# One hybrid decoder layer on one core: expert weights as 384 units in one ring of twenty buffers, experts written out

## The chip, the cores and the metric

The kernel runs on one core of a Trainium2 chip. The metric is the device time of one execution in microseconds, smaller being better. A profiled execution gives the trace from which the rows below are copied.

## The reference, cut to what matters

320 tokens (256 of a prompt, 64 new ones) of width 1024 go through one layer. A projection to seven parts of 1024 columns feeds two recurrent branches, whose merged result goes through `w_out` and a layer norm. Then a router picks 4 of 32 experts for each token, and a second layer norm closes the layer. Everything is float32. Each expert has a gate-and-up matrix of 1024 x 2048 (8 MB) and a down matrix of 1024 x 1024 (4 MB), so the 32 experts bring 384 MB from memory.

```python
proj = x @ w_in + b_in                       # 7 parts
... # two convolutions, a gated linear recurrence, gates
x = layernorm(ALPHA * x + mixed @ w_out, ln1_g, ln1_b)
top_vals, top_idx = lax.top_k(x @ router_w + router_b, 4)
gates = softmax(top_vals)
# for each expert e and each token row that chose it
gu   = xb @ w_gu[e] + b_gu[e]
gate = minimum(gu[:, :1024], 7.0)
up   = clip(gu[:, 1024:], -7.0, 7.0)
h    = (up + 1.0) * (gate * sigmoid(1.702 * gate))
y    = h @ w_down[e] + b_down[e]             # added to the token with its gate
x = layernorm(ALPHA * x + y_sum, ln2_g, ln2_b)
```

## The kernel before, in words

**Projection.** The first stage (0 to 230 us) makes 56 pieces of 128 output columns. A piece `q` is loaded (`raw`), rounded by ScalarE (`split_high`, L439), its remainder is taken by VectorE (`split_low`, L795), and TensorE multiplies it in three passes (L604). Seven pieces make a block `c` of 128 channels, and VectorE does the convolutions and the recurrence of the block in the same program order. There are four buffers of a piece. The product with `w_out` (L622) and the first norm follow, then the router.

**Experts.** Work comes in items: one expert with at most 64 rows. An expert with more rows gives more items; with these inputs there are just 32. A loop `one_pair(p)` runs over pairs of items on TensorE, VectorE and ScalarE, with the expert read from a list `items` by VectorE. For each item TensorE does, in this order:

- 64 matmuls of `w_gu` (L742; eight loads of 1 MB, called k, each used by eight matmuls of 128x512),
- one that spreads the row positions (L747),
- `gather` (L689): the rows of the *next* item, by a one-hot matrix that VectorE made in `pick` (L1016, L1017), after `low_part` (L1071) has taken the last result out of the same bank,
- `turn` (L695): four 128x128 transposes of the gathered rows, between two ScalarE copies (L529, L533),
- `turn_h` (L702): four transposes of the activated rows, reading every second column, then a ScalarE copy (L548),
- between these, `combine` (L710): the previous item's result back to token order, for VectorE to add (L833 with out `x_tok`),
- the bias (L762) and 32 matmuls of `w_down` (L769; four loads of 1 MB), then the next item's bias (L736).

VectorE clamps gate and up out of PSUM into the SBUF tile `mid` (L1088, L1089), ScalarE takes the tanh (L544), VectorE makes the product (L833 on `mid`).

**Weight buffers.** SyncE issues all loads from one queue in program order. There are 19 buffers of 1 MB: ten in `ring_gu`, `ring_last`, and eight in `ring_dn`. Even and odd items share the `ring_gu` buffers of k = 3 to 7 and own those of k = 0 to 2; each parity has four `ring_dn` buffers. `load_pair` issues in a fixed order, and a load whose buffer is not free holds back all behind it:

```python
for s in range(2):
    for k in range(KC) if early and s == 0 else (0, *gu_order[:-OWN], *range(1, OWN)):
        load_gu(experts[s], s, k, before * 16 + (16 + gu_count(0, k) if s == 1 and k >= OWN else
                                                 gu_count(1 if k >= OWN else s, k)))
    for u in range(4):
        sp.wait_ge(dn_used, before * 8 + (4 * s + u + 1))
        load_dn(experts[s], s, u)
```

The biases of all experts are loaded after `w_out` into `mid`, rounded by ScalarE (L502), and their remainder is taken by VectorE (L917) after the last block.

Of the kernel before, what the change touches and what calls it, by code (L numbers as in the profile page):

```python
# [24 lines left out]
OWN = 3  # L25
# [32 lines left out]
K_PAIR = 4  # L58
# [14 lines left out]
def hybrid_layer(nc, x_prompt, x_sample, state_h, state_conv, state_sc, w_in, b_in, conv_a_w,  # L73
# [5 lines left out]
    with ctx:  # L79
# [10 lines left out]
        slot = 8 * D  # L90
        GU, DN = 0, 10 * slot
        XT, X1 = DN + 8 * slot, DN + 8 * slot + 12 * D
        MID = X1 + 12 * D
        MID_SIZE = 4 * 3776
        at = [MID + MID_SIZE + 2 * slot]
# [14 lines left out]
        ring_gu = place("ring_gu", [P, 10, 2 * FF], GU)  # L110
        ring_dn = place("ring_dn", [P, 8, 2 * D], DN)

        def gu_slot(s, k):
            return KC + k if s == 1 and k < OWN else k

        ring_last = place("ring_last", [P, 2 * FF], MID + MID_SIZE + slot)

        def gu_tile(s, k):
            return ring_last[:, :] if gu_slot(s, k) == 10 else ring_gu[:, gu_slot(s, k)]

        gu_order = tuple(range(OWN, KC)) + tuple(range(OWN))

        def gu_count(s, k):

            return 8 * s + gu_order.index(k) + 1

        raw = place("raw", [P, RING, KC, P], DN)  # L130
        w_hi = place("w_hi", [P, RING, KC, P], DN + 2 * slot, F32R)
        w_lo = place("w_lo", [P, RING, KC, P], DN + 4 * slot, F32R)
        dsm = place("dsm", [P, 2 * D], DN + 7 * slot)
# [24 lines left out]
        x_hi = place("x_hi", [P, KC, T], MID, F32R)  # L158
        x_lo = place("x_lo", [P, KC, T], MID + 10 * D, F32R)
        mixT = place("mixT", [P, KC, T], MID + 20 * D)  # L160
# [3 lines left out]
        bias4 = place("bias4", [P, 3, HALF], MID + 28 * HALF, F32R)  # L164
        onehot = place("onehot", [P, 3, ROWS], MID + 20 * D)
        posT4 = place("posT4", [P, T], MID + 20 * D + 12 * ROWS, F32R)

        ident = small_tile("ident", [P, P])
        upper = small_tile("upper", [P, P])
        ones = small_tile("ones", [P, P])  # L170
        iota = small_tile("iota", [P, (NB + 1) * ROWS])
        rw = small_tile("rw", [P, KC, NE])
        esel4 = place("esel4", [P, 2, 2, ROWS], at[0] - 4 * KC * NE, F32R)
        rb = small_tile("rb", [P, NE])
        posm = small_tile("posm", [P, 3, NE])
        gate = small_tile("gate", [P, 3, NE])
        onehotT = small_tile("onehotT", [P, 2, T], F32R)
        where4 = small_tile("where4", [P, 2, NE])
        row_at = small_tile("row_at", [P, NB + 1])
        items = small_tile("items", [1, 2, 64], I32)  # L180
# [9 lines left out]
        tiles = place("tiles", [P, 12 * T + 2 * P], GU + 8 * slot)  # L190
# [18 lines left out]
        xg_sb, xgT_f = (mid[:, i * HALF:(i + 1) * HALF] for i in range(2))  # L209
        ys = place("ys", [P, 2, HALF], MID + 8 * HALF, F32R)  # L210
# [8 lines left out]
        gm, th, up = (mid[:, i * HALF:(i + 1) * HALF] for i in range(4, 7))  # L219
        bias_raw = mid[:, 4 * HALF:7 * HALF]  # L220
        pos4 = mid[:, 2240:2240 + 3 * P].rearrange("p (t a h e) -> p t a h e", t=3, a=2, h=2)
# [18 lines left out]
        oh4 = mid[:, 2240:2624].rearrange("p (t k e) -> p t k e", t=3, k=TOPK)  # L240
        og4 = mid[:, 2624:3008].rearrange("p (t k e) -> p t k e", t=3, k=TOPK)
# [10 lines left out]
        gu_in = [sem(f"gu_in{k}") for k in range(KC + OWN)]  # L252
        dn_in = [sem(f"dn_in{k}") for k in range(8)]
# [20 lines left out]
        gu_used, dn_used = sem("gu_used"), sem("dn_used")  # L274
# [11 lines left out]
        slot_out = ring_dn[:, 0:4, :].rearrange("p j (k n) -> p j k n", k=2)  # L286
        ln_g, ln_b = ring_dn[:, 6, 0:D], ring_dn[:, 6, D:2 * D]
        ln2g, ln2b = ring_gu[:, OWN, 0:D], ring_gu[:, OWN, D:2 * D]
# [3 lines left out]
        def _(sp):  # L292
            def load_piece(q):
                if q >= RING:
                    sp.wait_ge(lo_ok, q - RING + 1)
                col = ORDER[q % 7] * D + (q // 7) * P
                sp.dma_start(raw[:, q % RING], win_v[:, :, col:col + P]).then_inc(raw_in[q % RING], 16)

# [21 lines left out]
            for q in range(4, NP):  # L320
                load_piece(q)
                if q % 4 == 3 and q < 7 + 4 * KC:
                    k = (q - 7) // 4
                    sp.dma_start(ring_gu[:, k], w_gu[0, 0, k * P:(k + 1) * P, :]).then_inc(gu_in[k], 16)
            sp.dma_start(rw[:, :, :], router_w[0].rearrange("(k p) e -> p k e", p=P)).then_inc(misc_in, 16)
            sp.dma_start(rb[:, :], router_b[0:1, :].to_broadcast([P, NE])).then_inc(misc_in, 16)
            sp.dma_start(ln_g, ln1_g[0:1, :].to_broadcast([P, D])).then_inc(ln_in, 16)
            sp.dma_start(ln_b, ln1_b[0:1, :].to_broadcast([P, D])).then_inc(ln_in, 16)
            for j in range(4):
                if j < 2:  # L330
                    sp.wait_ge(lo_ok, NP - 2 + 2 * j)
                else:
                    sp.wait_ge(proj_done, NP - 6 + 2 * j)
                sp.dma_start(slot_out[:, j], wout_v[:, 2 * j:2 * j + 2, :]).then_inc(wout_in[j], 16)
# [9 lines left out]
            def load_gu(e, s, k, used=None):  # L344

                src = w_gu[0, ds(e, 1), k * P:(k + 1) * P, :].rearrange("a p n -> p (a n)")
                if used is not None:
                    sp.wait_ge(gu_used, used)
# [797 lines left out]
```

## Time and profile before

| what | us |
|---|---|
| median of three runs (1245.11 to 1254.6) | 1250.66 |
| the profiled execution's own time | 1256.6 |
| its span, first to last instruction | 1254.8 |
| TensorE busy | 1194.4 |
| VectorE busy | 526.6 |
| ScalarE busy | 254.3 |
| experts' first and last weight matmul | 295.9 to 1228.6 |
| bytes moved | 443.16 MB |

The own time lies 1.8 us above the span. The span has three parts: up to 295.9 us everything ahead of the experts, then the experts, and after 1228.6 us the last sums, the second norm and the stores (26.2 us). TensorE is busy nearly everywhere, but a busy TensorE can be one whose weights arrive just in time, so the stages have to be read one by one.

### The profile page before, as it was taken

To read this page: it belongs to the slowest core of one execution; us is meant where nothing else is said; L and a number is where in the kernel's file an instruction comes from. 1 tells how busy PE (TensorE), PEld (TensorE's weight loads), DVE (VectorE), ACT (ScalarE), POOL (GpSimd) and SP (SyncE) were. 2 spreads that over 40 slices of the span, in tenths; PEclk is the share of its full clock that TensorE was granted. 3 is DMA by queue.
4 is the path that set the end of the run, shared out by engine and by line. 5 is a ranking of instruction groups with operands and counts; after the bars stand their busy time and mean duration, and the time that the engine had idled before them with its cause. 6 is when DMAs were issued, how large, how long until landed. Compare 5 with 4: busy or idle time off the path is not lost.

```text
span 1254.8 us, 16159 instructions
## 1 busy us (share of the span) xinstructions
PE 1194.4 (95%) x5767; PEld 561.0 (45%) x5767; DVE 526.6 (42%) x991; ACT 254.3 (20%) x392; POOL 13.7 (1%) x16
## 2 busy tenths in 40 slices
PE   8999999899999999999999999999999999999992
PEld 7999999455333333333333333333333333333330
DVE  4788788565332233222333322332222233333326
ACT  3555655211111111111111111111111111111111
POOL 1000000000000000000000000000000000000003
PEclk8999999899999999999999999999999999999996
DMA  7666745837799999999999999999999999999991
GB/s 195 200 214 217 214 135 143 286 119 310 310 369 422 421 422 422 422 422 422 422 422 422 422 421 422 422 422 422 421 422 422 422 422 422 422 422 422 422 402 43
DMA packets 120147, 443.16 MB, mean 353 GB/s; under 512 B 10824, under 2 KB 68312, under 8 KB 70974
## 3 DMA queue, kind: packets, MB, share of 16 engines
q1 hardware_dynamic: 120030, 442.69, 88.5%
q8 instruction: 10, 0.16, 0.1%
q10 hardware_dynamic: 96, 0.22, 0.0%
q14 instruction: 11, 0.09, 0.0%
HBM read 441.34 MB, written 1.53 MB: 353 GB/s over the span
## 4 chain that ended last, share of the span: by engine, by line
PE 62%; DMA 14%; DVE 11%; ACT 6%; SPq 3%; issue 3%; DVEq 0%; ACTq 0%
PE PS L742 27%; PE PS L769 15%; DMA ring_gu<-in_w_gu 13%; PE PS L689 6%; PE PS L604 4%; SPq L349 3%; PE PS L622 3%; DVE w_lo L795 2%; DVE tiles L833 2%; PE PS L702 2%; PE PS L736 1%; PE PS L695 1%; ACT mid L529 1%; ACT mid L533 1%; ACT mid L548 1%
## 5 line engine op out<-in xcount | busy, mean ns | idle before, releaser
L742 PE MATMUL PS<-ring_gu,mid 128*64 128x512 f32 x1920 | 423.7, 595 | 6.6 <-DMA ring_gu<-in_w_gu 6.2
L742 PEld LDWEIGHTS PS<-ring_gu,mid 128*64 128x64 f32 x1920 | 133.1, 137 | 280.7 <-issue 249.6
L769 PE MATMUL PS<-ring_dn,mid 128*64 128x512 f32 x1024 | 226.8, 595 | 0.0
L1088 DVE TENSOR_SCALAR mid<-PS 128x512 f32<-128x512 f32 x32 | 22.1, 692 | 342.8 <-PE PS L742 342.8
L604 PE MATMUL PS<-x_hi,w_hi 128*128 128x320 f32 x448 | 141.6, 316 | 1.3 <-DVE w_lo L795 1.3
L604 PE MATMUL PS<-x_hi,w_lo 128*128 128x320 f32 x448 | 138.9, 310 | 0.0
L604 PE MATMUL PS<-x_lo,w_hi 128*128 128x320 f32 x448 | 138.9, 310 | 0.0
L1071 DVE TENSOR_TENSOR ys<-PS,ys 64x512 fp32r<-64x512 f32 x64 | 44.1, 688 | 223.8 <-ACT ys L551 223.3
L833 DVE SCALAR_TENSOR_TENSOR x_tok<-PS,gate,x_tok 128x1024 f32<-128x1024 f32 (+1 forms) x99 | 126.8, 1281 | 25.4 <-PE PS L710 21.5
L769 PEld LDWEIGHTS PS<-ring_dn,mid 128*64 128x64 f32 x1024 | 70.7, 137 | 135.6 <-issue 135.6
L544 ACT ACTIVATE mid<-mid 128x512 f32<-128x512 f32 x32 | 20.2, 631 | 462.1 <-DVE mid L1088 462.1
L689 PE MATMUL PS<-x,onehot 128*64 128x512 f32 (+1 forms) x396 | 97.1, 608 | 0.0
L551 ACT ACTIVATE ys<-PS 64x512 fp32r<-64x512 f32 x64 | 37.9, 592 | 244.4 <-PE PS L769 243.6
L604 PEld LDWEIGHTS PS<-x_hi,w_hi 128*128 128x128 f32 x448 | 84.6, 189 | 3.7 <-issue 3.1
L604 PEld LDWEIGHTS PS<-x_lo,w_hi 128*128 128x128 f32 x448 | 84.6, 189 | 0.6
L604 PEld LDWEIGHTS PS<-x_hi,w_lo 128*128 128x128 f32 x448 | 84.5, 189 | 0.0
L795 DVE TENSOR_TENSOR w_lo<-raw,w_hi 128x1024 fp32r<-128x1024 f32 x56 | 66.9, 1222 | 25.0 <-ACT w_hi L439 24.4
L710 PE MATMUL PS<-ys,onehotT 128*128 128x512 f32 (+1 forms) x198 | 69.5, 434 | 2.1 <-DVE ys L1071 2.1
L439 ACT ACTIVATE w_hi<-raw 128x1024 fp32r<-128x1024 f32 x56 | 58.9, 1051 | 7.0 <-DVE dsm L825 4.1
L689 PEld LDWEIGHTS PS<-x,onehot 128*64 128x64 f32 (+1 forms) x396 | 22.4, 134 | 50.9 <-issue 50.7
L833 DVE SCALAR_TENSOR_TENSOR mid<-mid 128x512 f32<-128x512 f32 x64 | 43.9, 686 | 1.1
L622 PE MATMUL PS<-ring_dn,mixT 128*128 128x512 f32 (+1 forms) x96 | 37.9, 636 | 3.6 <-DMA ring_dn<-in_w_out 3.6
(194 smaller groups left out, 722.2 us busy)
## 6 DMA issues: line engine op xcount, KB each, us to landing
ring_gu<-in_w_gu SPq DMA_DIRECT2D x240, 1024.0 KB, 22.4
ring_dn<-in_w_down SPq DMA_DIRECT2D x128, 1024.0 KB, 26.2
raw<-in_w_in SPq DMA_DIRECT2D x56, 512.0 KB, 4.7
ring_last<-in_w_gu SPq DMA_DIRECT2D x16, 1024.0 KB, 25.6
ring_dn<-in_w_out SPq DMA_DIRECT2D x4, 1024.0 KB, 6.0
x_tok<-in_x_prompt SPq DMA_DIRECT2D x1, 1024.0 KB, 6.8
out<-x SPq DMA_DIRECT2D x2, 512.0 KB, 2.8
ring_dn<-in_ln_g SPq DMA_DIRECT2D x1, 512.0 KB, 4.3
```

Source lines behind the costliest of these rows:

```text
L349: sp.dma_start(gu_tile(s, k), src).then_inc(gu_in[gu_slot(s, k)], 16)
L439: act.activation(w_hi[:, q % RING], raw[:, q % RING], ACT.Copy).then_inc(hi_ok, 1)
L551: act.activation(y_rows(a, 0), PS[64 * a:64 * a + 64, XB, :], ACT.Copy).then_inc(yhi_ok, 1)
L604: last = mm(PS[:, j % 6, 0:T], w[:, q % RING, k, :], x[:, k, :], start=(k == 0 and n == 0), stop=(k == KC - 1 and n == 2))
L622: last = mm(out, mixT[:, k, t0:t0 + n], slot_out[:, k // 2, k % 2, a * HALF:(a + 1) * HALF], start=(k == 0), stop=(k == KC - 1))
L689: last = mm(PS[64 * a:64 * a + 64, XB, :], onehot[0:n, t, :], x1[0:n, t, a * HALF:(a + 1) * HALF], start=(t == 0), stop=(t == 2))
L710: last = mm(PS[0:n, bank + a, :], onehotT[:, par, t0:t0 + n], ys[:, a, :], start=True, stop=True)
L742: last = mm(PS[64 * a:64 * a + 64, b, :], xgT[:, k % 4, k // 4, :], gu_tile(s, k)[:, (2 * b + a) * HALF:(2 * b + a + 1) * HALF], start=Fal ...
L769: last = mm(PS[64 * a:64 * a + 64, XB, :], hT[:, k % 4, k // 4, :], ring_dn[:, u, o:o + HALF], start=False, stop=(k == KC - 1))
L795: dve.tensor_tensor(w_lo[:, q % RING], raw[:, q % RING], w_hi[:, q % RING].bitcast(F32), ALU.subtract).then_inc(lo_ok, 1)
L833: return dve.scalar_tensor_tensor(out=out, in0=in0, scalar=scalar, in1=in1, op0=op0, op1=op1)
L1071: last = dve.tensor_tensor(y_rows(a, 1), PS[64 * a:64 * a + 64, XB, :], y_rows(a, 0).bitcast(F32), ALU.subtract)
```

## The change

1. The expert weights are 12 units of 1 MB per expert, 384 in all, in one ring of 20 buffers. They are loaded in the order of use; unit n waits for the use of unit n - 20. The 16 KB of two weight rows (`w_gu`) or four (`w_down`) per partition are read as two units of 8 KB each, so the rows of 8 KB that a unit reads lie 16 KB apart.
2. To fit these rows, `turn_x` reads every second column, and `turn_h` every fourth.
3. The experts are written out: 14, then a loop of two (it runs once, and again for items beyond 64 rows), then 16. The first of the last 16 is gathered again after the loop, since the loop gathered for the list.
4. Expert 0 has no `combine`; the last one has no `gather`, no `turn_x`. Indices of the written out experts are constants.
5. The clamps write back to PSUM (`gm`, `up` are banks 0 and 1); only `th` is in SBUF.
6. The biases are loaded ahead of piece 4, rounded by ScalarE at piece 8, and their remainder is taken by VectorE at the end of block 1.
7. Buffers are placed anew, with another order of the first loads; `ln1_b` is loaded after the last projection piece.

```diff
-        def gu_slot(s, k):
-            return KC + k if s == 1 and k < OWN else k
...
+        ring = place("ring", [P, SLOTS, WIDE], 0)
...
+            def rows_of_unit(n, e):
+
+                u, e = n % UNITS, ds(n // UNITS, 1) if e is None else ds(e, 1)
+                if u < KC:
+                    v = u // 2
+                    return w_gu[0, e, 2 * v * P:2 * (v + 1) * P, :].rearrange("a (p j) n -> p (a j) n", j=2)[:, u % 2, :]
+                v = (u - KC) // 2
+                return w_down[0, e, 4 * v * P:4 * (v + 1) * P, :]\
+                    .rearrange("a (p h j) n -> p h (a j n)", h=2, j=2)[:, u % 2, :]
...
+            sp.wait_ge(proj_done, NP)
+            load_unit(8)
+            load_unit(9)
+            sp.dma_start(ln_b, ln1_b[0:1, :].to_broadcast([P, D])).then_inc(ln_in, 16)
+            load_unit(12)
+            load_unit(13)
             sp.wait_ge(block_ok, KC + 1)
+            load_unit(10)
+            load_unit(11)
             sp.wait_ge(wout_done, 5)
+            for n in range(16, 20):
+                load_unit(n)
             sp.wait_ge(x1_ok, 3)
             sp.wait_ge(so_turned, 1)
+            load_unit(14)
+            load_unit(15)
+            for n in range(SLOTS, UNITS * (LOOP + 2)):
+                sp.wait_ge(used, n - SLOTS + 1)
+                load_unit(n)
...
+            for n in range(UNITS * (LOOP + 2), UNITS * NE):
+                sp.wait_ge(used, n_more * (2 * UNITS) + (n - SLOTS + 1))
+                load_unit(n)
...
             def turn_h(src, done):
 
-                for v in range(2):
-                    for j in range(2):
-                        last = pe.transpose(PS[:, TB, (2 * v + j) * P:(2 * v + j + 1) * P],
-                                            src[:, 2 * P * v + j:2 * P * (v + 1):2], ident[:, :])
+                for j in range(4):
+                    last = pe.transpose(PS[:, TB, j * P:(j + 1) * P], src[:, j:HALF:4], ident[:, :])
                 last.then_inc(done, 1)
...
+            for i in range(LOOP):
+                one_expert(i, 0)
+            with pe.Fori(0, n_loop) as it:
+                for i in range(LOOP, LOOP + 2):
+                    one_expert(i, it)
+            pe.wait_ge(ylo_ok, 2 * n_more + (LOOP + 2))
+            gather(2 * n_more + rows_in(LOOP + 2))
+            pe.wait_ge(xg_ok, 2 * n_more + rows_in(LOOP + 2))
+            turn_x(xg_sb, tx_done)
+            for i in range(LOOP + 2, NE):
+                one_expert(i, n_more)
...
+                if c == 1:
+                    dve.wait_ge(bias_hi, 1)
+                    for a in range(2):
+                        rows = slice(64 * a + 32, 64 * a + 64)
+                        whole = bias4[rows, :, :].rearrange("p b n -> p (b n)")
+                        last = dve.tensor_tensor(whole, bias_raw[rows, :], whole.bitcast(F32), ALU.subtract)
+                    last.then_inc(bias_ok, 1)
...
+                dve.tensor_scalar(gm, gm, LIMIT, None, ALU.min).then_inc(gm_ok, 1)
+                link(dve.tensor_scalar(up, up, LIMIT, -LIMIT, ALU.min, ALU.max))
...
+                link(stt(th, th, 1.0, gm, ALU.add, ALU.mult))
+                stt(th, up, 1.0, th, ALU.add, ALU.mult).then_inc(h_ok, 1)
```

## Rows read from the trace of the kernel before

**Rows 1.** The page: GB/s in 40 slices of the span.

```profile
GB/s 195 200 214 217 214 135 143 286 119 310 310 369 422 421 422 422 422 422 422 422 422 422 422 421 422 422 422 422 421 422 422 422 422 422 422 422 422 422 402 43
```

**Rows 2.** Chain of waits, first item and start of the second: start, us, what.

```profile
295.91 13.88 PE PS L742 x64
...
310.14 2.90 PE PS L689 x12
...
313.06 0.61 ACT mid L529
...
313.80 0.64 PE PS L695 x4
...
315.12 0.76 PE PS L702 x4
...
317.05 7.02 PE PS L769 x32
...
324.73 13.88 PE PS L742 x64
```

**Rows 3.** Chain of waits, items 19 to the last.

```profile
843.37 13.88 PE PS L742 x64
...
881.23 26.84 DMA ring_gu<-in_w_gu
...
940.95 26.85 DMA ring_gu<-in_w_gu
...
1179.67 27.51 DMA ring_gu<-in_w_gu
...
1221.57 7.04 PE PS L769 x32
```

**Rows 4.** Windows: from:to, length, busy us of the engines, PEclk, DMA share, GB/s.

```profile
239.50:250.00 10.50, 10.50 (x22) 3.72 (x22) 3.50 (x2) 1.48 (x1) 0.00 (x0) 0.74 0.98 373
...
320.00:325.00 5.00, 5.00 (x24) 1.64 (x22) 0.26 (x1) 0.86 (x2) 0.00 (x0) 1.00 0.02 10
325.00:330.00 5.00, 5.00 (x26) 1.72 (x24) 1.83 (x6) 0.32 (x1) 0.00 (x0) 1.00 0.45 159
```

**Rows 5.** Weight loads of the transposes L702 and L695: ns min/median/max.

```profile
L702 PEld LDWEIGHTS PS<-ident,mid x128: 195/209/218, 315.1 to 1220.0; 128*128 128x128 f32 x128
...
L695 PEld LDWEIGHTS PS<-ident,mid x132: 137/141/144, 293.7 to 1218.6; 128*128 128x128 f32 x132
```

**Rows 6.** Timeline, the end of item 0 on ScalarE and VectorE.

```profile
324.11 1.21 ACT L551 ACTIVATE ys<-PS 64x512 fp32r<-64x512 f32 x2 [7.61 <-PE PS L769]
...
324.74 1.39 DVE L1071 TENSOR_TENSOR ys<-PS,ys 64x512 fp32r<-64x512 f32 x2 [6.98 <-ACT ys L551]
...
326.65 0.22 DVE L1017 CAST esel<-where 128x128 fp32r x1
```

**Rows 7.** Timeline, VectorE's product of item 0.

```profile
311.74 1.41 DVE L833 SCALAR_TENSOR_TENSOR mid<-mid 128x512 f32<-128x512 f32 x2
```

**Rows 8.** Timeline, ScalarE in block 1, TensorE after `w_out` landed, and the biases.

```profile
59.16 0.53 ACT L472 ACTIVATE tiles<-PS,dsm 128x320 f32<-128x320 f32 x1 [5.72 <-DVE mixT L910]
...
239.50 32.56 PE L622 MATMUL PS<-ring_dn,mixT 128*64 128x512 f32 x72 [3.63 <-DMA ring_dn<-in_w_out]
...
243.96 1.48 ACT L502 ACTIVATE bias<-mid 128x1536 fp32r<-128x1536 f32 x1 [9.93 <-DMA mid<-in_b_down]
245.47 3.52 DVE L917 TENSOR_TENSOR bias<-mid,bias 32x1536 fp32r<-32x1536 f32 x2 [6.48 <-ACT bias L502]
```

**Rows 9.** Timeline of VectorE, the remainders of pieces 18 and 20.

```profile
85.53 1.22 DVE L795 TENSOR_TENSOR w_lo<-raw,w_hi 128x1024 fp32r<-128x1024 f32 x1
...
93.60 4.63 DVE L795 TENSOR_TENSOR w_lo<-raw,w_hi 128x1024 fp32r<-128x1024 f32 x4
```

**Rows 10.** Chain of waits, TensorE's piece 20 and piece 27.

```profile
94.95 3.78 PE PS L604 x24
...
121.10 3.78 PE PS L604 x24
```

More of the change, by code:

```diff
@@ L251, in hybrid_layer @@
         ln2_in = sem("ln2_in")
[L252 to L253 removed]
+        unit_in = [sem(f"unit_in{s}") for s in range(SLOTS)]
         const_ok, zero_ok, pool_own = sem("const_ok"), sem("zero_ok"), sem("pool_own")
@@ L691, in gather, with turn_x @@
                 last.then_inc(xg_done, 1)
-            def turn(src, done):
-                for j in range(4):
-                    last = pe.transpose(PS[:, TB, j * P:(j + 1) * P], src[:, j * P:(j + 1) * P], ident[:, :])
-                last.then_inc(done, 1)
-            def turn_h(src, done):
+            def turn_x(src, done):
                 for v in range(2):
@@ L703, in turn_h @@
                                             src[:, 2 * P * v + j:2 * P * (v + 1):2], ident[:, :])
+                last.then_inc(done, 1)
+            def turn_h(src, done):
+                for j in range(4):
+                    last = pe.transpose(PS[:, TB, j * P:(j + 1) * P], src[:, j:HALF:4], ident[:, :])
                 last.then_inc(done, 1)
@@ L781, in _ @@
+            gather(2 * n_more + rows_in(LOOP + 2))
+            pe.wait_ge(xg_ok, 2 * n_more + rows_in(LOOP + 2))
+            turn_x(xg_sb, tx_done)
+            for i in range(LOOP + 2, NE):
+                one_expert(i, n_more)
+            pe.wait_ge(ylo_ok, 2 * n_more + NE)
+            pe.wait_ge(c_taken, 6 * n_more + 3 * (NE - 1))
             for t, b in LAST_SUMS:
@@ new lines, in _ @@
+            n_loop = dve.value_load(pairs[0:1, 0:1], min_val=1, max_val=1 + MAX_EXTRA // 2)
+            n_more = dve.value_load(pairs[0:1, 1:2], min_val=0, max_val=MAX_EXTRA // 2)
+            for i in range(LOOP):
+                one_expert(i, 0, i - 1, row_at[:, 0:1], (i + 1,))
+            first = link.n
+            with dve.Fori(0, n_loop) as it:
+                link.off = it * 4
+                for i in range(LOOP, LOOP + 2):
+                    k = i - LOOP
+                    before, e = listed(2 * it + k), listed(2 * it + (k + 2))
+                    b_now, b = part(2 * it + (k + 1)), part(2 * it + (k + 2))
+                    one_expert(i, it, before, row_at[:, ds(b_now, 1)], (e, b))
@@ L1108, in _ @@
+            assert link.n - first == 4
+            link.off = n_more * 4
+            low_part(2 * n_more + (LOOP + 2))
+            dve.wait_ge(xg_done, 2 * n_more + (LOOP + 3))
+            pick(0, LOOP + 2)
+            e_last = listed(2 * n_more + 2)
+            for i in range(LOOP + 2, NE):
+                one_expert(i, n_more, e_last if i == LOOP + 2 else i - 1, row_at[:, 0:1], (i + 1,))
+            low_part(2 * n_more + NE)
             dve.wait_ge(ln2_in, 32)
             link = Chain(dve, dve_end)
-            e_end = expert(n_pairs * 2)
```

380 lines of the change are left out of this document (178 added, 202 removed).

## The prediction

> **What bounds the kernel now.** I read the page first, then the chain of waits, then windows over the places where the chain changes its character.
>
> The page shows TensorE busy for 1194.4 of 1254.8 us, which is 95%, and from about 380 us on, a transfer rate of 422 GB/s in nearly every slice [rows 1]. Both look like a bound, so the chain has to say which wait ends last. From 295.91 us each item is a closed row of TensorE steps and ScalarE copies, with no transfer in it, and the next item's first matmul starts at 324.73 [rows 2]: a period of 28.82 us set by TensorE. The chain reads like this for 20 items, the last of them starting at 843.37 [rows 3]. From then on a transfer stands in it every second item, at 881.23, 940.95 and so on to 1179.67 [rows 3]. Two of these are 59.72 us apart, so an item takes 29.86 us and 1 MB takes 59.72 / 24 = 2.49 us. The buffers carried TensorE for 20 items; 12 items are set by the transfers. TensorE's last weight matmul ends at 1221.57 + 7.04 = 1228.6 us [rows 3]. At TensorE's own pace it would be 295.9 + 32 x 28.82 = 1218.1 us. **So transfers cost 10.5 us in all**, and that is all that a better ring can give back.
>
> Where were the bytes lost? Between 320 and 325 us the transfer engines are idle (share 0.02), and until 330 us they move 159 GB/s in place of 422 [rows 4]: 4.9 + 3.1 = 8.0 us of transfer. SyncE's queue stood behind one load whose buffer was still in use, with other buffers free.
>
> **The change part by part**, against the span of 1254.8 us.
>
> *The ring.* In order of use, unit 20 can be issued once unit 0 is used, and then one unit follows each use. Eight uses in 13.88 us are more than the 5.6 units that can land meanwhile, so apart from perhaps 1 us before the first down unit the transfers never rest. That gives back 8.0 us, and one more buffer 2.5 us, less 1 us: the transfers alone would let TensorE end at about 1228.6 - 9.5 = 1219 us. The 1218.1 us of TensorE's pace and every term below come on TensorE's side, so TensorE sets all 32 items: **-10.5 us**. The last units will land some 15 us or more before their use.
>
> *The second gather after the loop.* When item 15 ends nothing of item 16 is ready, and a row of steps which is otherwise hidden lies bare. From the end of L769 (317.05 + 7.02 = 324.07 [rows 2]) the low part ends at 324.74 + 1.39 = 326.13, and `pick` at 326.65 + 0.22 = 326.87 [rows 6]: 2.8 us until the gather may start. Then 2.90 for the gather, 0.74 for the copy up to the next transpose (313.06 to 313.80), 0.76 for transposes with a stride of two, and 0.67 for the copy [rows 2]: 7.9 us, and the loop's end on top, **+8.0** (7 to 9). Transfers run on meanwhile, but nothing waits for them.
>
> *The last expert* has no gather, copies and transposes of x. But then VectorE's product is next: it ends at 311.74 + 1.41 = 313.15 us [rows 7], where `turn_h` started at 315.12 [rows 2]. The gain is **-1.9**, not the 4.9 us of the steps. Expert 0's missing `combine` gives 0: it stood beside ScalarE's copies.
>
> *The transposes of x* get the form which `turn_h` has now: 0.76 for 0.64 us [rows 2], with weight loads of 209 for 141 ns [rows 5]. 32 times 0.12: **+3.8**.
>
> *The transposes of h* read every fourth column. No row shows this. From one side it costs nothing more than a stride of two. From the other, take the load's time as growing with the stretch of memory it crosses: 141 to 209 ns for twice the stretch gives 209 + 2 x 68 = 345 ns for four times. The first load then adds 0.136 us, and the three behind it, which overlap, perhaps 0.07 each: 0.35 us; I allow 0.5. I take 0.15 per expert, nearer to the row that is there than to a straight line through two: **+4.8** (0 to 16).
>
> *The biases.* VectorE's two operations of 3.52 us in all [rows 8] move from a place beside the `w_out` product to the end of block 1. There VectorE is just in time: pieces 20 and 27 start on TensorE at 94.95 and 121.10 [rows 10], so a piece takes about 26.15 / 7 = 3.74 us with its share of the block's other work, and piece 18 starts at about 87.5. Its remainder is ready at 86.75, that of piece 20 at about 94.8 [rows 9]. Delayed by 3.52 us, they stop TensorE for some 2.8 us at piece 18 and a total of **+3.3** at piece 20 (0 to 5). Behind VectorE's two operations stand all the remainders, and TensorE waits for these. ScalarE's 1.48 us [rows 8] falls into a wait of 5.72 us for the end of block 0 [rows 8], at nothing. The eight issues stand ahead of piece 4 and all later pieces on SyncE. TensorE reaches piece 4 only after four pieces of 3.7 us, so I count 0 (to 2).
>
> *The clock.* After 3.63 us without work, ended by the landing of `w_out` [rows 8], the granted clock was 0.74 over the next 10.5 us, which is a part of them at 1.2 GHz instead of 2.4 [rows 4]. The second gather and the biases bring 2.8 us of rest each. If the clock falls there it costs 2 to 3 us each. I take **+2.0** for both (0 to 6).
>
> *The rest at nothing.* The clamps in PSUM lie on VectorE, whose product is ready 1.97 us before `turn_h` starts (313.15 to 315.12) [rows 2, 7]; only more than 2 us would show. The written out code: the step from one item to the next shows no gap in the chain, so there is no loop cost to save. `ln1_b` now lands behind two more units: 239.5 + 2.5 x 2.49 = 246 us, while VectorE came to it only after its work on the biases, which ended at 249.0 [rows 8]. Preloads 14 and 15 come last, but are used only by expert 1.
>
> Sum: -10.5 + 8.0 - 1.9 + 3.8 + 4.8 + 3.3 + 2.0 = **+9.5 us**. The span becomes 1264.3 and the execution's own time 1256.6 + 9.5 = 1266.1, a ratio of 1.0076. The profiled execution was 0.5% above the median; the median of 1250.66 becomes **1260**.
>
> **The rivals.**
>
> *A, a stride of four is free and the bias is covered* (not slower). For it: the step from one to two cost only 0.12 us of the path, and where VectorE is late it may have idle time ahead. The sum is then -10.5 + 8.0 - 1.9 + 3.8 = -0.6, with either one remaining up to +4: 1250 to 1255. Against: piece 20's remainder is ready 0.2 us before TensorE starts the piece [rows 9, 10].
>
> *B, the stride costs by the stretch or more.* 0.35 to 0.5 us, 32 times, is 11 to 16 in place of 4.8: 1266 to 1271, and 1275 with the clock. By the rule of the skill cited above this would be the result, as the first stride beyond its limit; the line of 345 ns has the same sign.
>
> *C, the transfers become the bound again.* Rows of 8 KB at a distance of 16 KB, or the written out code fetched over the same engines, slow them. TensorE's last matmul after the change (1228.6 + 9.5 = 1238) is some 16 us behind what transfers allow (1219 and the 3.3 us of the biases), and 364 units take 364 x 2.49 = 905 us, so it decides only from 16 / 905 = 1.8% on; at 4% it adds 36 - 16 = 20 us: about 1280. Against: both matrices stream at 422 GB/s now, whatever their place.
>
> *D, faster.* The ring's 10.5 us come in full and the item gets shorter, since constants replace computed addresses and PSUM operands free a port. For 1% it needs 0.4 us less per item even with A true. The only candidate in the chain is the 0.13 us between copy and transpose (313.67 to 313.80 [rows 2]); all of it is 4 us: about 1246. Against: no address work stands in the chain.
>
> **How the numbers follow.** The forecast 0.45, A 0.22, B 0.21, C 0.04, D 0.08. Changes below about 1% can hardly be told from none in this kernel. Over 1% slower is above 1263.2: B, C and a quarter of the forecast's own case, 0.36. Faster by 1% is D at most, 0.07. The range goes from D's edge at 1246 to 1275, which leaves out C and the far end of B.
>
> **What would show it.** In the profile of the changed kernel: no transfer in the chain between items; a period of 29.0 to 29.2 us, with `turn_x` at 0.76 and `turn_h` at about 0.9; a gap of some 8 us after item 15; remainders (L795) ending a wait of TensorE at 88 to 98 us; the first weight matmul at about 299 us; transfers at 422 GB/s without a hole at 320 us. A period of 28.9 makes A right, one of 29.3 B, and a transfer in the chain C. I am wrong altogether if the item has a step which I hold for fixed and which the new order shortens.

## The result, and the profile after

The kernel after took 1257.85 us (median of 5 runs, 1254.36 to 1259.12) beside 1250.62 us for the kernel before (5 runs): a ratio of 1.006, 95% interval 1.0031 to 1.0089. A second set, 12 runs of the kernel after beside 17 of before, gave 1.0028 (1.0008 to 1.0047). So the change costs some 3.5 to 7 us, 0.3 to 0.6%; 1260 had been forecast. The profiled execution took 1254.36 us, its span was 1252.6 us.

The transfers, GB/s in 40 slices, of the page after; each slice is 31.3 us:

```profile
GB/s 246 233 185 208 195 134 152 322 204 269 384 422 421 421 420 421 421 420 421 422 421 421 421 420 422 421 421 421 421 420 422 422 420 421 421 421 421 421 226 42
```

The chain of waits of the kernel after, from the landing of `w_out` over expert 0, one expert of the middle, and the last (start, us, what):

```profile
227.12 7.70 DMA ring<-in_w_out
234.95 29.95 PE PS L632 x72
...
289.33 13.88 PE PS L758 x64
...
310.70 8.51 PE PS L790 x32
...
319.87 13.88 PE PS L758 x64
...
339.16 0.77 PE PS L714 x4
...
341.10 7.02 PE PS L790 x32
...
348.78 13.88 PE PS L758 x64
...
1196.85 13.88 PE PS L758 x64
...
1216.88 9.41 PE PS L790 x32
```

`DMA` never stands between two experts now, where in [rows 3] it did every second item. An expert takes 348.78 - 319.87 = 28.91 us from first matmul to first matmul. It was 28.82 in [rows 2] where no transfer bound, and 29.86 in [rows 3] where one did. Two rows are longer than their like: expert 0's down product with 8.51 us and the last one's with 9.41, where 7.02 us is usual. Expert 0 also starts at 289.33, not at 295.91 [rows 2].

The chain between items 15 and 16, the second gather:

```profile
745.89 7.04 PE PS L790 x32
...
752.96 0.60 ACT ys L551
...
753.58 0.67 DVE ys L1108
...
755.77 2.97 PE PS L699 x12
...
758.76 0.61 ACT mid L526
...
759.41 0.76 PE PS L707 x4
...
760.19 0.60 ACT mid L530
...
762.07 14.97 PE PS L758 x64
```

From 752.93 to 762.07 TensorE waits at each step for ScalarE or VectorE: 9.14 us, where `combine` alone (0.67 us) stands between other items. The gate and up product behind it takes 14.97 in place of 13.88 us.

Windows of the kernel after (columns as in [rows 4]), on the clock in expert 0 and on the transfers at 320 us:

```profile
305.00:310.00 5.00, 2.89 (x14) 1.31 (x12) 1.43 (x3) 1.79 (x3) 0.00 (x0) 1.00 1.02 429
310.00:315.00 5.00, 4.95 (x15) 1.60 (x17) 0.00 (x0) 0.00 (x1) 0.00 (x0) 0.66 0.69 290
320.00:325.00 5.00, 5.00 (x25) 1.58 (x22) 1.97 (x6) 0.46 (x1) 0.00 (x0) 1.00 1.01 401
325.00:330.00 5.00, 5.00 (x26) 1.72 (x24) 0.00 (x0) 0.00 (x0) 0.00 (x0) 1.00 1.00 419
```

The hole in the transfers is gone: 401 and 419 GB/s where [rows 4] has 10 and 159. In expert 0, which has no `combine` to fill the waits for ScalarE's copies, TensorE works only 2.89 of 5 us, and over the next 5 us the granted clock is 0.66: most of them at 1.2 GHz instead of 2.4.

The weight loads of the transposes of x (L707, stride two) and of h (L714, stride four), ns min/median/max:

```profile
L707 PEld LDWEIGHTS PS<-ident,mid x132: 194/209/218, 286.5 to 1186.1; 128*128 128x128 f32 x132
L714 PEld LDWEIGHTS PS<-ident,mid x128: 196/212/220, 308.6 to 1214.4; 128*128 128x128 f32 x128
```

A stride of four costs 3 ns more than a stride of two; the stride of two costs 68 ns more than none [rows 5].

Where the span went, by stages in us, worked out from the matmuls' start and end records: the start up to the first piece's matmul; the pieces (L614); the `w_out` product; norm and router up to the first expert weight matmul; the experts up to the end of the last down product; the tail.

| kernel | start | pieces | w_out | norm, router | experts | tail | span |
|---|---|---|---|---|---|---|---|
| before | 20.3 | 209.2 | 42.6 | 23.8 | 932.7 | 26.3 | 1254.8 |
| before_again | 17.4 | 210.0 | 40.9 | 24.7 | 932.3 | 26.3 | 1251.5 |
| after | 15.0 | 212.1 | 37.8 | 24.4 | 937.0 | 26.3 | 1252.6 |
| after_again | 15.0 | 213.0 | 37.8 | 24.4 | 936.9 | 26.3 | 1253.4 |
| one_list | 17.2 | 213.5 | 37.5 | 25.6 | 925.6 | 25.8 | 1245.1 |
| bias_gap | 14.3 | 208.5 | 37.0 | 24.4 | 935.6 | 25.8 | 1245.5 |
| busy_ends | 19.2 | 213.7 | 37.7 | 24.4 | 934.4 | 25.8 | 1255.2 |
| plain_rows | 14.7 | 213.4 | 37.8 | 24.4 | 934.2 | 25.8 | 1250.2 |
| three | 14.6 | 209.4 | 37.9 | 26.0 | 923.3 | 25.8 | 1237.0 |
| all_four | 14.8 | 209.0 | 37.6 | 24.6 | 921.5 | 25.8 | 1233.3 |

The rows from one_list on are told with the experiments. The start differs by up to 6 us between profiles (before and before_again, the same program, are 2.9 apart), so single spans are not compared below; stages and timed ratios are. The kernel before and half_down start at 17.4 to 20.3 us, the eleven profiles of the changed kernel and its variants at 14.3 to 19.2; whether the new order of the first loads has a part in that was not tested. Without the start, the mean of the two profiles of after is 3.7 us above the mean of the two of before, which answers to the timed 3.5 of the larger set.

### The profile page after: what moved, and what is told of

It is laid out like the page before. It is cut to its first block, busy times and chain, and to the rows that moved or that the text cites. A ratio compares the mean times of both kernels' runs of the same rounds, so it can differ in the third digit from the quotient of the medians.

```text
span 1252.6 us, 14341 instructions
## 1 busy us (share of the span) xinstructions
PE 1192.6 (95%) x5761; PEld 564.6 (45%) x5761; DVE 521.7 (42%) x988; ACT 252.9 (20%) x392; POOL 13.4 (1%) x16
## 4 chain that ended last, share of the span: by engine, by line
PE 79%; DVE 11%; ACT 7%; issue 3%; DMA 1%; DVEq 0%; POOL 0%; ACTq 0%; POOLq 0%
PE PS L758 36%; PE PS L790 18%; PE PS L699 7%; PE PS L614 5%; PE PS L632 2%; PE PS L707 2%; PE PS L714 2%; DVE w_lo L827 2%; PE PS L752 2%; DVE tiles L865 2%; ACT mid L526 2%; ACT mid L530 2%; ACT mid L548 1%; PE PS L785 1%; DVE tiles L929 1%
## 5 line engine op out<-in xcount | busy, mean ns | idle before, releaser
L758 PE MATMUL PS<-ring,mid 128*64 128x512 f32 x2048 | 447.6, 595 | 0.0
L758 PEld LDWEIGHTS PS<-ring,mid 128*64 128x64 f32 x2048 | 144.4, 137 | 286.9 <-issue 286.9
L790 PE MATMUL PS<-ring,mid 128*64 128x512 f32 x1024 | 230.6, 603 | 0.0
L1121 DVE TENSOR_SCALAR PS<-PS 128x512 f32<-128x512 f32 x32 | 22.4, 699 | 384.5 <-PE PS L758 384.5
L614 PE MATMUL PS<-x_hi,w_hi 128*128 128x320 f32 x448 | 141.7, 316 | 3.8 <-DVE w_lo L827 3.8
L614 PE MATMUL PS<-x_hi,w_lo 128*128 128x320 f32 x448 | 139.1, 310 | 0.0
L614 PE MATMUL PS<-x_lo,w_hi 128*128 128x320 f32 x448 | 139.0, 310 | 0.0
L790 PEld LDWEIGHTS PS<-ring,mid 128*64 128x64 f32 x1024 | 71.6, 139 | 139.3 <-issue 139.3
L865 DVE SCALAR_TENSOR_TENSOR x_tok<-PS,gate,x_tok 128x1024 f32<-128x1024 f32 (+1 forms) x96 | 122.9, 1281 | 27.4 <-PE PS L721 24.3
L543 ACT ACTIVATE mid<-PS 128x512 f32<-128x512 f32 x32 | 19.1, 597 | 454.6 <-DVE PS L1121 454.6
L551 ACT ACTIVATE ys<-PS 64x512 fp32r<-64x512 f32 x64 | 37.9, 591 | 249.5 <-PE PS L790 248.7
L614 PEld LDWEIGHTS PS<-x_hi,w_hi 128*128 128x128 f32 x448 | 84.7, 189 | 6.3 <-ACT tiles L474 3.1
L614 PEld LDWEIGHTS PS<-x_lo,w_hi 128*128 128x128 f32 x448 | 84.8, 189 | 0.6
L614 PEld LDWEIGHTS PS<-x_hi,w_lo 128*128 128x128 f32 x448 | 84.7, 189 | 0.0
L827 DVE TENSOR_TENSOR w_lo<-raw,w_hi 128x1024 fp32r<-128x1024 f32 x56 | 66.9, 1222 | 24.4 <-ACT w_hi L435 23.9
L721 PEld LDWEIGHTS PS<-ys,onehotT 128*128 128x128 f32 (+1 forms) x192 | 27.2, 181 | 30.2 <-issue 27.6
L632 PE MATMUL PS<-ring,mixT 128*128 128x512 f32 (+1 forms) x96 | 35.3, 597 | 1.5 <-DMA ring<-in_w_out 1.5
```

The costliest lines, as they stand in the source:

```text
L551: act.activation(y_rows(a, 0), PS[64 * a:64 * a + 64, XB, :], ACT.Copy).then_inc(yhi_ok, 1)
L614: last = mm(PS[:, j % 6, 0:T], w[:, q % RING, k, :], x[:, k, :], start=(k == 0 and n == 0), stop=(k == KC - 1 and n == 2))
L632: last = mm(out, mixT[:, k, t0:t0 + n], slot_out[:, k // 2, k % 2, a * HALF:(a + 1) * HALF], start=(k == 0), stop=(k == KC - 1))
L721: last = mm(PS[0:n, bank + a, :], onehotT[:, par, t0:t0 + n], ys[:, a, :], start=True, stop=True)
L758: last = mm(PS[64 * a:64 * a + 64, b, :], xgT[:, u % 4, u // 4, :], w[:, o:o + HALF], start=False, stop=(u == KC - 1))
L790: last = mm(PS[64 * a:64 * a + 64, XB, :], hT[:, 2 * (u % 2) + j, u // 2, :], w[:, j * D + a * HALF:j * D + (a + 1) * HALF], start=False, ...
```

## The experiments

**What does the ring alone give?** Half of the down matrices' bytes are left out of the kernel before, for items 2 to 31:

```diff
-            def load_dn(e, s, u):
+            def load_dn(e, s, u, part=False):
+                if part:
+                    sp.dma_start(ring_dn[:, 4 * s + u, 0:D], ...
...
-                        load_dn(experts[s], s, u)
+                        load_dn(experts[s], s, u, True)
```

> The kernel before, with only the first 4 KB of each partition's 8 KB loaded for the down matrices of items 2 to 31 (the second half holds what was there; this part of the computation is wrong). Theory 1 (transfers cost the experts' stage 10.5 us): all periods are 28.81 us and the stage goes from 932.5 to 922 us, the end of the change's ring gain. Theory 2 (something else lengthens the last 11 items): periods of 29.8 us remain there.

Measured: 1242.76 us, one run; the kernel computes wrong values, since it leaves out half of the down weights. The experts stage took 921.4 us, 11.1 less than 932.5 (mean of two of before). In the chain no transfer is left; three late items:

```profile
1013.68 13.88 PE PS L747 x64
...
1042.49 13.88 PE PS L747 x64
...
1071.31 13.88 PE PS L747 x64
```

28.81 us apart, to the last. The transfers cost the kernel before 11 us in this stage, and TensorE's own period is 28.81 us throughout. The last item takes 28.22 us here and 29.94 in the kernel before.

**The second gather.** One list of items for all 32 experts, so that the gather and transposes for item 16 run beside item 15, as for every other item:

```diff
-            return i + 1 if i < LOOP + 2 else i + 2
+            return i + 1
...
-            pe.wait_ge(ylo_ok, 2 * n_more + (LOOP + 2))
-            gather(2 * n_more + rows_in(LOOP + 2))
-            pe.wait_ge(xg_ok, 2 * n_more + rows_in(LOOP + 2))
-            turn_x(xg_sb, tx_done)
...
-                if i > 0 and i != LOOP + 2:
+                if i > 0:
```

> The changed kernel without the second gather: the list that the loop reads names expert 16 behind its last entry, so the loop's last pass gathers for expert 16, and the steps after item 15 are ordinary. Theory 1 (the bare row of steps between item 15 and item 16 costs its length): the stretch from item 15's last weight matmul to item 16's first falls from 9.1 us to 0.7, the granted clock no longer falls there, and the experts' stage is 9 to 10 us shorter; ratio to the kernel before about 0.998. Theory 2 (transfers are close behind): part of the 9.6 us comes back as waits of TensorE for units near the end, since the last units landed 14 to 17 us ahead of their use; then the gain is under 5 us. I hold to theory 1: 14 us are more than 9.6.

Measured: 0.9957 of before (0.994 to 0.9975), 1244.36 us. The chain at the same place:

```profile
750.40 7.02 PE PS L789 x32
757.42 0.67 PE PS L751 x2
758.08 13.88 PE PS L757 x64
```

The row of steps is gone and the weight matmuls keep 13.88 us. Both items around take 28.92 us, where after had 37.41 and 30.00. This one edit turns the change from slower into faster than before. The experts' stage is 11.4 us shorter than in after (925.6 for 937.0): 9.6 us of it are these two items, 1.9 us the last item (27.59 us for 29.48), whose clock is looked at further down. The pause itself costs more where the clock falls for longer behind it: items 15 and 16 together take 67.4 to 67.5 us in after, after_again, bias_gap and stride8, 68.9 and 69.0 in plain_rows and busy_ends and 71.1 in small_behind, where 57.8 us would be two ordinary items (57.6 in plain_rows). That is 9.6 to 13.3 us.

The other side: the transfers had caught up during the pause. Counted over all units from the landings, the closest is the last gate-and-up unit of the last expert. It lands 0.8 us ahead of its use here and 10.6 us in after, not the 14 us of the expectation. Another 1 us, and this kernel would have waited for transfers.

**The biases.** Their remainders are taken in halves, one in the middle of block 1 and one in the middle of block 2, where VectorE waits about 2 us for ScalarE, ahead of the remainder of the next piece:

```diff
+                if c in (1, 2):
+                    rows = slice(64 * (c - 1) + 32, 64 * (c - 1) + 64)
+                    ...   # this half's subtraction
+                    dve.tensor_tensor(whole, bias_raw[rows, :], ..., ALU.subtract).then_inc(bias_ok, 1)
...
-                    for a in range(2):
-                        ...   # both halves in block 1
```

> The changed kernel with the two operations on the biases' remainders taken apart and put ahead of piece 7c+10's remainder in blocks 1 and 2, where VectorE waits about 2 us for ScalarE. Theory 1 (they cost because all remainders stand behind them): the stage from piece 0 to the last piece goes from 208.3 us to about 205, 3 us less in all, and no L827 ends a wait of TensorE of more than 0.2 us; no clock drop near 84 us. Theory 2 (the stage lost its 2.9 us elsewhere, by the early transfers of the biases ahead of piece 4): nothing changes, 208 us.

Measured: 0.9994 (0.9977 to 1.0011), 1249.35 us; pieces stage 208.5 us in place of 212.1 and 213.0. In the chain of the kernel after the two operations stand whole, with TensorE waiting behind them:

```profile
78.69 1.75 DVE bias L949
80.45 1.75 DVE bias L949
...
82.65 1.24 DVE w_lo L827
84.01 6.05 PE PS L614 x29
```

All of TensorE's waits for remainders between 15 and 232 us (total us, times, longest), after and then bias_gap:

```profile
PE PS L614 <- DVE w_lo L827: 3.8, 7, 2.8
```

```profile
PE PS L614 <- DVE w_lo L827: 1.1, 6, 0.2
```

One wait of 2.8 us at piece 18 is gone, and with it a fall of the clock. The window behind that wait, after and then bias_gap:

```profile
84.00:95.00 11.00, 10.99 (x64) 11.00 (x65) 10.53 (x26) 3.33 (x5) 0.00 (x0) 0.84 0.68 225
```

```profile
84.00:95.00 11.00, 10.89 (x71) 10.32 (x70) 8.96 (x19) 5.52 (x10) 0.00 (x0) 1.00 0.93 282
```

So the bias step costs 3.6 to 4.5 us, clock included. With both operations in block 1 the stage takes 212.1 to 214.0 us in eight profiles; with them apart, 208.5 to 209.4 us in three.

**Is it the clock at the two ends?** Eight small matmuls on data at hand fill TensorE's waits in expert 0 and in the last, and compute nothing that is used:

```diff
+            def fill(i, it, n):
+                if i in (0, NE - 1):
+                    for _ in range(n):
+                        mm(PS[:, XB if i else 7, 0:P], ident[:, :], ident[:, :], start=True, stop=True)
```

(3 ahead of the wait for the transposed one-hot, 2 ahead of that for h, 3 after `turn_h`.)

> The changed kernel with eight small extra matmuls in expert 0 and in the last expert, where combine or gather are missing; they compute nothing that is used. Theory 1 (the rests that the removed steps leave lower the granted clock): no stretch of 1.2 GHz near 310 and near 1214 us; expert 0 takes 28.9 us instead of 30.5, the last one's down matmuls 7.0 us instead of 9.4; 3 to 4 us less in all. Theory 2 (the clock falls there for other reasons, as it does in some runs anyway): the stretches stay, and nothing is gained, or the extra matmuls cost 0.5 to 1 us.

Measured: 1.0028 (1.0005 to 1.0051), 1254.73 us. Expert 0 begins at 295.05 here; the windows over its filled waits and over its down product, and then the chain with both down products in question:

```profile
309.00:316.00 7.00, 6.31 (x37) 3.68 (x37) 3.12 (x5) 2.22 (x4) 0.00 (x0) 1.00 1.01 424
316.00:323.00 7.00, 6.98 (x33) 2.41 (x34) 0.00 (x0) 0.17 (x1) 0.00 (x0) 1.00 0.93 332
```

```profile
316.72 7.02 PE PS L799 x32
...
1222.34 7.04 PE PS L799 x32
```

The granted clock stays at 1.00, and the products take 7.02 and 7.04 us in place of 8.51 and 9.41. Expert 0 takes 29.35 us in place of 30.54, the last 26.42 in place of 29.48: 4.3 us between these two profiles. The second gather cost 1.6 us more in this execution (39.01 + 30.01 for 37.41 + 30.00), so the stage gained 2.6 us, 0.2%. The timed ratio equals that of after's second set and lies 0.3% under the first's: the times alone settle nothing on so little.

The other profiles say how far this holds. Expert 0 takes 30.5 to 31.8 us in all eight profiles without the extra matmuls and 29.3 to 29.4 in all three with them, so the 1.2 us are the waits' doing. The last item takes 26.4 to 29.5 us in the eight without. In plain_rows and stride8 nothing is filled, and yet its product keeps the full clock:

```profile
1217.34 7.04 PE PS L788 x32
```

So the waits of the last item can lower the clock but need not. What the extra matmuls give back there is 0 to 3.1 us, and what decides it stays open.

**The strides.** Units of whole rows as before, so x is transposed side by side and h with a stride of two:

```diff
-                    return w_gu[0, e, 2 * v * P:2 * (v + 1) * P, :].rearrange("a (p j) n -> p (a j) n", j=2)[:, u % 2, :]
+                    return w_gu[0, e, u * P:(u + 1) * P, :].rearrange("a p n -> p (a n)")
...
-                    last = pe.transpose(PS[:, TB, j * P:(j + 1) * P], src[:, j:HALF:4], ident[:, :])
+                        last = pe.transpose(..., src[:, 2 * P * v + j:2 * P * (v + 1):2], ident[:, :])
```

> The changed kernel with the rows of a unit as in the kernel before (1 MB in one piece), so that the transposes of x read columns side by side and those of h every second one. Theory 1 (0.1 us per expert is the stride-two form of the transposes of x, and nothing else): the period goes from 28.91 to 28.82 us, 3 us in all, and the transfer rate stays at 422 GB/s. Theory 2 (the distance of 16 KB between rows costs transfer rate): the rate rises above 422 GB/s, and units land earlier before their use than 14 us at the end. Theory 3 (a stride of four costs more than a stride of two): the period falls below 28.7.

Measured: 1.0007 (0.999 to 1.0024), 1250.17 us. The chain, transposes of x, transposes of h, and two starts:

```profile
812.37 0.64 PE PS L704 x4
...
813.68 0.76 PE PS L711 x4
...
823.30 13.88 PE PS L756 x64
...
852.12 8.30 PE PS L756 x37
```

The period is 852.12 - 823.30 = 28.82 us for 28.91, 2.9 us over 32 items. It all comes from x: 0.64 us for 0.73 to 0.76. For h the step is 0.76 with a stride of two and 0.76 to 0.77 with four. The stage as a whole (934.2 for 937.0 us) is no measure of it: the last item is 3.0 us shorter here, expert 0 and the second gather are 1.3 and 1.5 us longer, and all three go with the clock. The transfer rate was 421 GB/s in both kernels between 400 and 1000 us: to read 8 KB rows at a distance of 16 KB costs nothing against rows that lie side by side.

Does the cost grow at all beyond that? The transposes of x read every eighth column of `mid` (other numbers, same count):

```diff
-                            src[:, 2 * P * v + j:2 * P * (v + 1):2], ident[:, :])
+                            mid[:, j:2 * HALF:8], ident[:, :])
```

> The changed kernel, with the transposes of x reading every eighth column of a range twice as wide, which includes old data (the values that the experts get are wrong, all else is as before). Theory 1 (a load costs 141 ns side by side and about 210 for any larger stride): the transposes' weight loads stay at 209 to 212 ns and the period at 28.91. Theory 2 (the cost grows with the stride beyond four): loads of 250 to 350 ns and a period of 29.0 to 29.2.

Measured: 1254.15 us, one run, period 28.875 us. The weight loads:

```profile
L706 PEld LDWEIGHTS PS<-ident,mid x132: 185/193/208, 290.9 to 1189.5; 128*128 128x128 f32 x132
```

193 ns is less than the 209 of a stride of two, so neither theory has it quite. Side by side costs 141 ns, and strides of two, four and eight 209, 212 and 193.

**What is the ring's depth worth?** The change with ten of its twenty buffers:

```diff
-                sp.wait_ge(used, n - SLOTS + 1)
+                sp.wait_ge(used, n - SLOTS + 1 + 10)
```

> The changed kernel, with the load of every unit from 20 on waiting for ten more uses, as if the ring had ten buffers. Theory 1 (the ring's depth pays the difference between TensorE's 28.91 us and the transfers' 29.85 us per expert, and 14 us of it were left over): ten buffers less are 24.9 us, so about 11 us of waits for units appear in the last third, the experts' stage goes from 937 to about 948 us, and the period turns to 29.85 us there. Theory 2 (the order of use was the gain, depth is not needed): no wait for units, 937 us.

Measured: 1272.68 us, one run; experts stage 952.4 us, 15.4 more than after. The period is 28.91 us for items 1 to 9, then 29.83 to 29.89 up to the second gather, again 28.91 for items 17 to 23, 31.40 for item 25, and 29.80 to 29.84 behind it. TensorE's waits for units (total us, times, longest), and the chain at the gather:

```profile
PEld PS L758 <- DMA ring<-in_w_gu: 35.8, 41, 1.6
...
PE PS L758 <- DMA ring<-in_w_gu: 8.4, 15, 0.8
```

```profile
728.78 16.85 DMA ring<-in_w_gu
...
774.16 15.68 PE PS L758 x64
```

Transfers need 12 x 2.49 = 29.88 us for an expert and TensorE 28.91, so every expert uses up about 1 us of the lead; the buffers hold the lead. The pause of the second gather refills it. Added up over the gate-and-up products, the waits for units come to 13.7 us. Ten buffers less are 24.9 us, and with the lead of 10.6 us that after has left this would be 14.3; the expectation's 11 came from a lead of 14. Some 3.7 us more are a longer low clock at the gather (41.32 + 30.71 us for 37.41 + 30.00, of which 0.9 is a wait for units; small_behind, with all its buffers, has 40.43 + 30.70), and the last item's down product is 1.9 us shorter than after's.

**The `w_out` stage**, where the change is 3 to 5 us faster, was in no step of the forecast. One thing that moved: before, the small transfers of the biases stood behind `w_out`'s. The kernel after with eight such extra transfers put right behind them, into a free buffer:

```diff
+            for a in range(2):
+                for h in range(2):
+                    rows = slice(64 * a + 32 * h, 64 * a + 32 * h + NE)
+                    ...   # b_gu, b_down -> ring[rows, 12, ...], .then_inc(extra_in, 16)
...
+            sp.wait_ge(extra_in, 128)   # ahead of load_unit(12)
```

> The changed kernel, with the eight small loads of the biases issued a second time where the kernel before has them, right behind the last piece of w_out (into a buffer that is free; unit 12 waits for them). Theory 1 (these small transfers share the engines with w_out and delay it): TensorE waits 3 to 4 us for w_out instead of 1.5, the clock falls behind it, and the w_out stage goes from 37.8 to 41 to 42.6 us. Theory 2 (the stage is shorter after the change for another reason, such as the work that left ScalarE and VectorE): it stays at 37.8.

Measured: 1259.62 us, one run. The window of this kernel, then that of the kernel after, then that of before_again, the kernel before in its second profile:

```profile
235.00:240.00 5.00, 2.84 (x9) 1.11 (x10) 2.26 (x8) 0.00 (x0) 0.00 (x0) 1.00 1.09 210
```

```profile
235.00:240.00 5.00, 5.00 (x14) 2.04 (x15) 1.51 (x5) 0.00 (x0) 0.00 (x0) 1.00 0.98 387
```

```profile
235.00:240.00 5.00, 3.37 (x6) 1.06 (x7) 1.79 (x5) 0.00 (x0) 0.00 (x0) 0.68 1.06 280
```

The engines are full in the first two (share 1.09 and 0.98), yet with the small transfers they move 210 GB/s and not 387. `w_out` lands later, TensorE's wait for it is 2.87 us for 1.49, and the stage takes 39.2 us for 37.8. The kernel before waits 3.63 us in its first profile [rows 8] and 2.89 in its second. So the wait is 1.4 to 2.1 of the 3 to 5 us. The rest is the product behind it: 32.56 us [rows 8] and 31.60 in the two profiles of before, 29.95 in after and in small_behind. It runs on a lower clock in before (0.74 in [rows 4], 0.68 above) and on the full one in small_behind, behind a wait of the same 2.9 us. Why the clock falls in the one and not in the other stays open.

**Again, both.** The unchanged kernels once more, beside the others:

> The kernel before, unchanged, for a second profile. In the first its w_out stage took 42.6 us, with a wait of 3.6 us for w_out and a low clock behind it, against 37.4 to 37.8 in four profiles after the change. If the small bias transfers behind w_out cause this, it is 42 to 43 us again; if it was chance, 37 to 38. The start of the first piece (20.3 us in the first, 14.3 to 19.2 in the others) should vary without the kernel.

> The changed kernel once more, unchanged, for its stages in a second profile and its time beside the same runs of the kernel before. If the single edits' sizes are right (9.6 for the second gather, against a ratio of 0.9957 without it), its ratio is 1.003 to 1.005, at the lower end of the first measurement's interval; if the first measurement's 1.006 stands, the second gather costs 12 us or more and I have missed some of it. Stages: pieces 212, w_out 37.8, experts 937.

Measured: 1253.29 us for before (one run), and for after the second set told in the result, 1.0028, just under the 1.003 to 1.005 that the sizes gave. The `w_out` stage of before took 40.9 us, between the two forecasts: the wait is there again and the low clock is shorter. All stages but the start repeat within 1.7 us. In the two profiles of after, expert 0's and the last one's long down products repeat too.

**Together.** one_list, bias_gap, busy_ends and plain_rows in one kernel, and the same without plain_rows:

> All four single edits in one kernel: no second gather, the biases' remainders in VectorE's waits, extra matmuls in expert 0 and the last one, rows as in the kernel before. Theory 1 (the costs are separate and add): the experts' stage is about 932.7 + 0.1 - 10.5 + 1 = 923 us, the stage of the pieces 208 to 209, the w_out stage 37.5; 12 to 15 us less than the kernel before, ratio 0.989. Theory 2 (transfers bind again once TensorE is that much faster): without the second gather units landed only 4.6 us ahead of their use, and 3 us of these go to the shorter period and 1 to 2 to expert 0; then one or two waits of TensorE for a unit stand near the end, and the ratio is 0.991 to 0.993.

> As all_four, but with the rows of the changed kernel (8 KB rows at 16 KB, strides two and four). Theory 1: 32 x 0.1 = 3 us more than all_four. Theory 2 (transfers bind): the same time as all_four, since the slower period leaves the slack that the other one lacks.

Measured: 0.9897 of before for both (0.9869 to 0.9926 and 0.9868 to 0.9926), 1239.33 and 1238.92 us. They beat the kernel before by 13 us and, by the ratios, the change by 16 to 20 us (one_list alone beats before by 5). By the times plain rows add nothing on top. The waits in all_four, and its chain at the last item:

```profile
PEld PS L761 <- DMA ring<-in_w_gu: 3.4, 4, 1.4
```

```profile
1166.75 26.17 DMA ring<-in_w_gu
...
1200.43 7.04 PE PS L796 x32
```

With a period of 28.82 us and no pause the twenty buffers run out near the end: four weight loads wait for units, 3.4 us together. The items show 1.1 us of it (the last takes 27.51 us, the one ahead of it 28.92). In `three` (28.91) one weight load waits 0.3 us, and the last item takes 26.51. So the transfers take back about 1.1 of the 2.9 us of the stride. In the profiles all_four's experts' stage is 1.8 us shorter than that of `three` (921.5 for 923.3), which the timed ratios, with intervals of 0.3% to either side, cannot tell from nothing.

## Why the prediction was right, and where its steps were not

The sum was +9.5 us; the stages show +3.7, the two timed sets +3.5 and +7.2. The sign, the kind and the range held, but several steps were off and cancelled, so that the sum came as near as it did is in part luck.

- **Ring, -10.5.** Right: half_down shows 11.1, and no transfer is left in after's chain. TensorE's pace held for 21 items of the kernel before, not 20, at no change to the sum. The "some 15 us or more" of lead are 16.3 for the last unit of all, but 10.6 for the last gate-and-up unit.
- **Second gather, +8.0.** Right: 9.14 - 0.67 = 8.5 us, and the clock adds 14.97 - 13.88 = 1.1. one_list, which takes away this and nothing else, gives the 9.6 back. In other executions of the same steps the clock made it 11 to 13.
- **Last expert, -1.9.** The mechanism was right and is hidden. busy_ends shows 26.42 us against 28.91 - 0.67 = 28.24: -1.8. plain_rows and stride8 have it too (26.44 and 26.42), without extra matmuls. In the two profiles of the change itself it is 29.48 and 29.46, 1.2 us more than the 28.22 of half_down, with the down product at 9.41 us on a low clock. Why the clock falls there in some executions and not in others is not shown.
- **Expert 0, 0.** Failed: +1.6 us, of which the extra matmuls give 1.2 back; the other 0.4 stay open. "It stood beside ScalarE's copies" was true of the path and not of the clock.
- **Transposes of x, +3.8.** Right: 0.09 to 0.10 us per item, 3 us.
- **Transposes of h, +4.8.** Mis-sized: 0.01 us per item, 0.3 us. I took a middle between "no dearer than two" and a line through two points; the first was true. Rival A had this half right, and the period of 28.91 is its mark. With the biases kept, its sum is -0.6 + 3.3, and 1253.4 lies nearer to the second set's 1254.7 than 1260 does. The Trainium skill (SBUF — State Buffer, Door 1: The DMA port swizzle, its note on cachelines) asks for two hits in a line of 16 bytes, by which fp32 at a stride of two would be free and dearer reads begin beyond it. The same note also gives "4 fp32" as how far one can stride for free, so "beyond the rule's limit in either reading" said more than the note does. The measured loads of 141, 209, 212 and 193 ns for strides of one, two, four and eight put the step at two and show none behind it, which fits neither; the measurement decides, and rival B's second ground falls with it.
- **Biases, +3.3.** Right in place (piece 18) and size: bias_gap gives 3.6 to 4.5 back, of which part is the clock counted elsewhere. The wait came 3.5 us earlier than forecast, in a kernel that started 5.3 us earlier.
- **Clock, +2.0.** Too low and partly in other places: 1.1 us behind the gather, 1.2 in expert 0, and in the two profiles of the change 3.1 in the last item; the share in the pieces stage stands in the bias term.
- **PSUM clamps and written out code, 0.** As said: L1121 takes 699 ns and is not in the chain, and the period without the strides is 28.82 us as before.
- **`w_out` stage, absent.** -3.9 us. I followed the eight bias issues to their new place and asked what they delay there, not what they stop delaying at the old one. small_behind shows 1.4 us of it as a shorter wait; the rest is the product on the full clock, whose cause is open.

In short, the gather, the clock and expert 0 came out some 4 us dearer than forecast, and h (4.5), `w_out` (3.9), x (0.8) and the ring (0.6) some 10 us better; by the stages the forecast was 6 us too high. The two largest misses are a size (h) and a stage that the sum left out (`w_out`). Rival D's shorter item is not there, and C's bound comes only in kernels faster than the change (all_four) or with half the buffers.

## What to carry to other kernels

A deeper ring pays only down to the other engine's own pace, and here its 11 us were nearly spent on a pause of 9.6 us which the restructuring brought in itself: when a loop is split, keep the preparation of the first item behind the seam inside the last item ahead of it. Work that is taken off TensorE can cost time, as in expert 0; look at what it stood beside, and at the granted clock right behind the place, in more than one profile. When a transfer is moved, ask also what it stood next to before.

## What the runs showed of the hardware

- A 128x128 fp32 weight load takes 141 ns side by side, 209 at a stride of two, 212 at four, 193 at eight.
- TensorE's granted clock fell behind short waits: 0.66 over 5 us behind a stretch in which it worked 2.89 of 5 us (expert 0), and stayed at 1.00 once eight small matmuls filled the same waits. It fell at expert 0 in eight profiles of eight without them, but for the last expert's product in six of eight, and not behind the 2.87 us of small_behind's `w_out`. Where it fell it cost from 0.4 us (one_list's last product) to about 4.8 (small_behind's second gather).
- With eight small transfers issued behind the 1 MB ones of `w_out`, the engines moved 210 for 387 GB/s at a full share, and `w_out` came 1.4 us later.
- 8 KB rows at a distance of 16 KB stream at 421 GB/s, as 8 KB rows side by side do (after and plain_rows, 400 to 1000 us).
- The first 15 to 20 us of a profile varied by 6 us, more than most effects told here.
